# Low parts of split attention weights on VectorE, and weight buffers that live across three stages of a streaming encoder step

## Chip, cores and metric

The kernel runs on one core of a Trainium2 chip. The metric is the time of one execution on the device, in microseconds. It is given as the median of several runs; one further execution is profiled, and its rows are those quoted here.

## The reference, cut to what matters

One layer of an encoder is computed for 1024 prompt rows and 32 sample rows, width 1024. A combined projection of `h` feeds a gated DeltaNet mixer (8 heads of 128), a banded softmax attention (8 heads of 64, computed here as 4 pairs) and two gates; then come a merge, a residual norm and a mixture of experts.

```python
proj = h @ w_in
y_a = gdn_mixer(u_a, z_a, b_a, a_a, ...)          # per head, per chunk:
    # rhs = [beta * v, beta * exp(G) * k];  sol = solve(I + M, rhs)
    # q_dec = q * exp(G);  k_dec = k * exp(G_last - G)
y_b = band_attention(qb, kb, vb, rel_bias)        # softmax(q k / 8 + bias) v
mix = sigmoid(g_a) * (y_a @ w_up_a) + sigmoid(g_b) * (y_b @ w_up_b)
x = layer_norm(ALPHA * x + (1 + gt1) * (mix @ w_out))
x = layer_norm(ALPHA * x + (1 + gt2) * moe(x * (1 + sc2) + sh2))
```

The projection is made in split precision: each operand is a high part (rounded) plus a low part (operand minus high part), and a product is three matmuls, high by high, low by high, high by low.

## The kernel before

The program is a row of phases, each a block in which the five engines run their own instruction lists and at whose end they meet: entry (norm, modulation), DeltaNet (`phase_deltanet`), attention (`phase_attention`), merge (`phase_merge`), residual, dispatch, experts. Nothing of a phase starts before all engines and the awaited stores of the one before have ended.

**Projection jobs.** A weight block of 128 columns is a job. SyncE loads it into `wraw`, ScalarE rounds it into the high part (`high`), GpSimd or VectorE subtracts (`low`), and TensorE multiplies it into 3 column groups of 352 rows, 8 steps each, 24 steps in all; a step is `split_matmul` (lines 138 to 144), three matmuls. In DeltaNet `wraw` is one buffer and the pairs `w2` are two, used in turn. The list `jobs` (lines 417 to 425) has the z block of head h and the k, q, v blocks of head h + 2 in turn; the last three jobs are the blocks k, q, v of attention's pair 0. `by_vector` and `by_pool` (lines 428 to 431) say which engine subtracts which job. SyncE may load job w only when job w - 1 has been subtracted (line 556).

**A DeltaNet head.** A round h (from -1 to 7) has 9 slots, the scan of head h over 9 tiles, and beside them the preparation of head a = h + 1; then a list of 13 stages `A2` (line 434) in which TensorE multiplies 9 tiles of 128 x 128 each and VectorE or ScalarE combines the results, three tiles (384 columns) at a time. TensorE puts product steps between slots and between stages (`slot_steps`, `stage_steps`, `run(fill, n)`). In the stages VectorE takes, in this order, BT, T_V (weighted values `bv`, which is `ET`), B2, Y, W, B4, W4, the transposed outputs T_O, and QK; in BT, B2 and B4 it also squares, sums and scales the outputs of head h (lines 1132 to 1147). GpSimd makes the decayed keys `kd` and the scaled keys `kt` (`scaled_keys`, lines 779 to 789; WK needs them), the decayed queries in `WE` (`queries`, lines 791 to 796; the next scan needs them), and low parts between these.

**Attention.** For each pair, TensorE computes scores of a tile, VectorE adds the bias and takes the maximum (`soft`), ScalarE exponentiates, VectorE normalises (`norm`), TensorE transposes and multiplies by v. Beside pair p TensorE runs the products of pair p + 1, two steps at each of four places of a tile; beside the last pair it runs modulation steps instead, whose weights come through a ring of 11 buffers, 7 of them loaded early. At the start ScalarE copies the transposed v in three parts and rounds a weight after each (lines 1440 to 1442):

```python
for j in range(NJ):
    take_v(0, j)
    high(1, j)
```

TensorE may start the scores of tile 1 only when both maxima of tile 0 are taken (line 1509), and the transposes of a tile only when it is normalised (line 1526). GpSimd subtracts all 9 weights (lines 1460 to 1466). SyncE's list starts at line 1343: bias rows, tables of pair 0, the three weights of pair 1, caches.

**Merge.** 16 gate jobs and 16 up-projection jobs, with two raw buffers and two split pairs of their own; weights are loaded, rounded and subtracted in halves. The first product waits for the first half of job 0 (line 1745).

## Time and profile before

| | us |
|---|---|
| median of 3 runs | 2026.38 |
| lowest and highest | 2022.24, 2026.57 |
| the profiled execution, its own time | 2018.53 |
| its span, first to last instruction | 2016.7 |
| TensorE busy in the span | 1811.6 |
| VectorE busy | 1006.6 |
| ScalarE busy | 662.1 |
| GpSimd busy | 219.7 |
| mean granted TensorE clock (share of full) | 0.945 |

DeltaNet takes the span from about 69 to 876 us, attention from 876 to 1156, the merge from 1156 on. PE is TensorE's matmuls, DVE is VectorE, ACT is ScalarE, POOL is GpSimd, SP is SyncE, and SPq and POOLq their queues. Busy time is no proof of a bound: the wait in brackets behind a row says how long the engine had stood idle before it and on whose result it waited.

### The profile page before, as it was taken

Reading aid. Unit: us, or ns where it says so; the run is one execution under the profiler, and the core shown is the slowest. Engines: PE = TensorE matmul, PEld = TensorE weight load, DVE = VectorE, ACT = ScalarE, POOL = GpSimd, SP = SyncE. Lnnn points to the kernel's source line nnn. Section 1 sums busy time; section 2 is a strip of 40 time slices with the busy share of each in tenths; the row PEclk is TensorE's granted clock in tenths of the full one; section 3 lists DMA queues with packets and bytes.
Section 4 is the critical chain, followed back from the end, with each engine's and each line's share of the span. In section 5 each row is a group of like instructions: output and inputs, shape, how many; then the busy total and the mean of one; then the engine's idle time right before and its main releaser. Section 6 shows DMA issues by size and latency. Waiting matters only on the chain. (4 is left out here: it accounts for less than half of the span.)

```text
span 2016.7 us, 29278 instructions
## 1 busy us (share of the span) xinstructions
PE 1811.6 (90%) x11059; PEld 1536.6 (76%) x11060; DVE 1006.6 (50%) x2211; ACT 662.1 (33%) x1297; POOL 219.7 (11%) x180
## 2 busy tenths in 40 slices
PE   5889999999999998989998799998988957999991
PEld 2689999999999997977876399998976844444440
DVE  5555757474665757334444411124438972333336
ACT  3454444535353544234444322222111110110104
POOL 0101101120202021110000000000000001222220
PEclk8899999999999999989999999999989977999995
DMA  9311020101011020130232622113124345888766
GB/s 351 116 37 46 22 70 25 57 25 58 35 47 56 26 70 14 34 126 2 77 119 102 217 83 95 43 32 117 43 96 191 112 177 223 303 246 271 225 166 203
DMA packets 69166, 219.67 MB, mean 109 GB/s; under 512 B 8596, under 2 KB 14380, under 8 KB 64948
## 3 DMA queue, kind: packets, MB, share of 16 engines
q1 hardware_dynamic: 61412, 190.20, 26.3%
q0 software_dynamic: 7632, 27.79, 5.6%
q8 instruction: 83, 1.36, 0.3%
q14 instruction: 39, 0.32, 0.0%
HBM read 178.11 MB, written 42.48 MB: 109 GB/s over the span
## 5 line engine op out<-in xcount | busy, mean ns | idle before, releaser
L142 PE MATMUL bk<-hT_high,w_high 128*128 128x352 f32 x840 | 297.2, 354 | 1.1 <-DVE ssq L1191 1.1
L144 PE MATMUL bk<-hT_high,w_low 128*128 128x352 f32 x840 | 273.5, 326 | 0.0
L143 PE MATMUL bk<-hT_low,w_high 128*128 128x352 f32 x840 | 273.5, 326 | 0.0
L2400 PE MATMUL psU<-wgu,xgT 128*128 x400 | 178.9, 601 | 2.1 <-DVE xgT L2487 2.1
L142 PEld LDWEIGHTS bk<-hT_high,w_high 128*128 128x128 f32 x840 | 162.3, 193 | 1.5 <-DVE ssq L1191 1.2
L143 PEld LDWEIGHTS bk<-hT_low,w_high 128*128 128x128 f32 x840 | 162.3, 193 | 0.0
L144 PEld LDWEIGHTS bk<-hT_high,w_low 128*128 128x128 f32 x840 | 160.5, 191 | 0.0
L2400 PEld LDWEIGHTS psU<-wgu,xgT 128*128 128x128 f32 x400 | 76.9, 193 | 99.3 <-issue 99.3
L142 PE MATMUL pg<-hT_high,wx_high 128*128 128x352 f32 x384 | 124.7, 325 | 9.9 <-DVE wx_low L1804 9.9
L1804 DVE TENSOR_TENSOR wx_low<-wx,wx_high 128x512 fp32r<-128x512 f32 (+1 forms) x64 | 37.4, 622 | 186.2 <-ACT wx_high L1782 182.9
L143 PE MATMUL pg<-hT_low,wx_high 128*128 128x352 f32 x384 | 123.6, 322 | 0.0
L144 PE MATMUL pg<-hT_high,wx_low 128*128 128x352 f32 x384 | 123.5, 322 | 0.0
L986 DVE SCALAR_TENSOR_TENSOR f<-raw,cw,f 128x1059 f32<-128x1059 f32 x72 | 97.1, 1348 | 9.3 <-ACT f L644 8.7
L2347 POOL TENSOR_TENSOR wait_cell<-wait_cell 128x1 f32<-128x1 f32 x27 | 18.2, 672 | 666.8 <-DVE idx L2472 666.8
L2436 ACT ACTIVATE sgx<-psU 128x256 f32<-128x256 f32 x25 | 9.6, 386 | 242.0 <-PE psU L2400 242.0
L2417 PE MATMUL psD<-wdn,aTx 128*128 x192 | 87.4, 598 | 0.0
L2493 DVE TENSOR_TENSOR ab<-psU,sgx 128x256 f32<-128x256 f32 x25 | 10.6, 425 | 151.5 <-ACT sgx L2436 151.5
L142 PEld LDWEIGHTS pg<-hT_high,wx_high 128*128 128x128 f32 x384 | 72.6, 189 | 10.8 <-DVE wx_low L1804 10.8
L142 PE MATMUL pja<-hT_high,wa_high 128*128 128x352 f32 x216 | 80.2, 372 | 0.4 <-POOL wa_low L1465 0.4
L142 PE MATMUL py<-wo_high,mix_high 128*128 128x512 f32 (+1 forms) x144 | 59.0, 409 | 19.4 <-DVE wo_low L2007 11.5
L143 PEld LDWEIGHTS pg<-hT_low,wx_high 128*128 128x128 f32 x384 | 72.7, 189 | 0.0
L144 PEld LDWEIGHTS pg<-hT_high,wx_low 128*128 128x128 f32 x384 | 72.4, 189 | 0.0
(430 smaller groups left out, 4018.1 us busy)
## 6 DMA issues: line engine op xcount, KB each, us to landing
wgu<-in_w_gu SPq DMA_DIRECT2D x16, 2048.0 KB, 9.2
wraw<-in_w_gdn SPq DMA_DIRECT2D x32, 512.0 KB, 3.6
wdn<-in_w_dn SPq DMA_DIRECT2D x16, 1024.0 KB, 13.3
wm<-in_w_mod SPq DMA_DIRECT2D x8, 1024.0 KB, 8.0
tmp_x<-x SPq DMA_DIRECT2D x16, 512.0 KB, 6.1
wx<-in_w_gates SPq DMA_DIRECT2D x32, 256.0 KB, 3.8
spare<-in_w_mod SPq DMA_DIRECT2D x12, 512.0 KB, 8.6
Dm<-tmp_g_rows SPq DMA_DIRECT2D x8, 576.0 KB, 4.1
```

The lines of the kernel that those rows point to most:

```text
L142: pe.matmul(out, lh, rh, start=start, stop=False)
L143: pe.matmul(out, lh, rl, start=False, stop=False)
L144: return pe.matmul(out, ll, rh, start=False, stop=stop)
L986: ins = dve.scalar_tensor_tensor(out=f[b][:, 0:CONVW], in0=raw[b][:, k:k + CONVW], scalar=cw[:, a, b, k:k + 1], in1=f[b][:, 0:CONVW], op0= ...
L1804: dve.tensor_tensor(lo[:, half(j, h), :], raw[j % 2][:, half(j, h), :], plain(hi[:, half(j, h), :]), ALU.subtract).then_inc(w_split, 1)
L2347: pool.tensor_tensor(waits[:, 0:1], waits[:, 1:2], waits[:, 1:2], ALU.add).then_inc(pdone, 1)
L2400: mm = pe.matmul(psU[b][:, :], xgT[b][:, i, :], c.wgu[:, bass.ds(place, 1), i, :].rearrange("p a c -> p (a c)"), start=(i == 0), stop=(i = ...
L2417: mm = pe.matmul(psD[:, h * 512:(h + 1) * 512], aT[b][:, i, :], c.wdn[:, bass.ds(place, 1), i, h * 512:(h + 1) * 512].rearrange("p a c -> ...
L2436: act.activation(sg[b][:, :], psU[b][:, 0:DE], ACT.Silu).then_inc(sgd, 1)
L2493: dve.tensor_tensor(ab[b][:, :], psU[b][:, DE:2 * DE], sg[b][:, :], ALU.mult).then_inc(a, 1)
```

## The change

Four things are changed.

1. In the DeltaNet stages VectorE makes the decayed keys (in stage T_V), the scaled keys (in Y) and the decayed queries (in W4), each behind its own combination, and the low part of the third weight of a round in W. GpSimd keeps its small fills and the low part of a round's last weight.
2. DeltaNet gets one more job to prepare, not to multiply: the first weight of attention's pair 1. It is loaded, rounded by ScalarE and subtracted by GpSimd in the last round, in buffer pair `c.ahead` (35 jobs, so pair 1).
3. `wraw` and the two pairs `w2` are allocated so that they live through attention and merge; attention uses them for two of its three weights, the merge for its jobs. Attention's other low parts are VectorE's, behind `norm` and `out` of tiles 0 and 1 (pair 0) and 3, 6, 9 (pairs 0 and 1).
4. In the last pair the first gate weight is loaded into `wraw`, rounded and subtracted, in attention; the merge starts with job 1's loads. The modulation ring has 10 buffers, 6 of them loaded early.

```diff
--- before.py
+++ after.py
@@ -423,12 +423,15 @@
     NSUB = NJ * len(jobs)
+    NEXT = len(jobs)
+    c.ahead = NEXT % 2
     EARLY = 2
...
     in_slots = [first_job[h] + 1 for h in range(-1, HA - 1)]
-    in_stages = [first_job[h] + 2 for h in range(-1, HA - 1) if first_job[h] + 2 <= first_job[h + 1]]
-    by_vector = sorted(in_slots + in_stages)
-    by_pool = [w for w in range(EARLY, len(jobs)) if w not in by_vector]
+    after_stage = {"BT": 2, "W": 3}
+    by_vector = sorted(in_slots + [first_job[h] + n for h in range(-1, HA - 1) for n in after_stage.values()
+                                   if first_job[h] + n < first_job[h + 1] + (n == 2)])
+    by_pool = [w for w in range(EARLY, NEXT + 1) if w not in by_vector]
 
@@ -554,8 +557,8 @@
                         weights_split(sp, w - 1)
-                    head, b = jobs[w]
-                    sp.dma_start(wraw[:, :, :], d["w_gdn"][head, b] if head < HA else d["w_att"][0, b]).then_inc(s["w_raw"], 16)
+                    head, b = jobs[w] if w < NEXT else (HA + 1, VB)
+                    sp.dma_start(wraw[:, :, :], d["w_gdn"][head, b] if head < HA else d["w_att"][head - HA, b]).then_inc(s["w_raw"], 16)
 
@@ -572,7 +575,7 @@
                 for h in range(-1, HA):
-                    w, end = first_job[h] + 1, min(first_job[h + 1], len(jobs) - 1)
+                    w, end = first_job[h] + 1, first_job[h + 1]
                     if w <= end:
@@ -601,7 +604,7 @@
 
-                    if w >= len(jobs):
+                    if w > NEXT:
                         return
@@ -763,7 +766,7 @@
                 def low(w):
-                    if w >= len(jobs):
+                    if w > NEXT:
                         return
@@ -775,25 +778,6 @@
                     pool.memset(X[:, :, :].rearrange("p i j -> p (i j)")[:, 0:BS * BS:BS + 1], 1.0).then_inc(s["x_one"], 1)
-
-                def scaled_keys(a):
-                    evacuated(pool, a, "T_K")
-                    evacuated(pool, a, "BT")
-                    if a > 0:
-                        pool.wait_ge(s["ds"], NCHUNK * a)
-                    pool.tensor_tensor(by_tile(kd), by_tile(kt), tok(a, Q_KD).unsqueeze(2).to_broadcast([P, TILES, P]),
-                                       ALU.mult).then_inc(s["kd"], 1)
-                    pool.wait_ge(s["kd"], a + 1)
-                    pool.wait_ge(s["cols"], a + 1)
-                    pool.tensor_tensor(by_tile(kt), by_tile(kt), col[:, 2, :].unsqueeze(2).to_broadcast([P, TILES, P]),
-                                       ALU.mult).then_inc(s["kb"], 1)
-
-                def queries(a):
-
-                    pool.wait_ge(full[NGRP - 1], use[a, "W4", NGRP - 1] + 1)
-                    pool.wait_ge(s["actv"], 3 * a + 2)
-                    pool.wait_ge(s["eg_in"], 16 * (a + 1))
-                    pool.tensor_tensor(WE[:, :, P:2 * P], by_tile(f[QB]), by_tile(EG), ALU.mult).then_inc(s["eq"], 1)
 
@@ -804,13 +788,9 @@
                     blocks(a)
-                    scaled_keys(a)
-                    if w + 3 <= end:
-                        low(w + 2)
-                    queries(a)
                     if w + 2 <= end:
                         low(end)
-                for w in range(first_job[HA - 1] + 1, len(jobs)):
+                for w in range(first_job[HA - 1] + 1, NEXT + 1):
                     low(w)
@@ -1106,8 +1086,6 @@
                                                   ALU.add).then_inc(free[g], 1)
-                            if first_job[a - 1] + 2 in in_stages:
-                                low(first_job[a - 1] + 2)
                         if name == "T_V":
@@ -1129,6 +1107,22 @@
                             combine(a, "QK", PT, Dm, ALU.mult)
+                        if name == "T_V":
+                            evacuated(dve, a, "T_K")
+                            if a > 0:
+                                dve.wait_ge(s["ds"], NCHUNK * a)
+                            dve.tensor_tensor(by_tile(kd), by_tile(kt), tok(a, Q_KD).unsqueeze(2).to_broadcast([P, TILES, P]),
+                                              ALU.mult).then_inc(s["kd"], 1)
+                        if name == "Y":
+                            dve.wait_ge(s["kd"], a + 1)
+                            dve.wait_ge(s["cols"], a + 1)
+                            dve.tensor_tensor(by_tile(kt), by_tile(kt), col[:, 2, :].unsqueeze(2).to_broadcast([P, TILES, P]),
+                                              ALU.mult).then_inc(s["kb"], 1)
+                        if name == "W4":
+                            dve.wait_ge(full[NGRP - 1], use[a, "W4", NGRP - 1] + 1)
+                            dve.wait_ge(s["actv"], 3 * a + 2)
+                            dve.wait_ge(s["eg_in"], 16 * (a + 1))
+                            dve.tensor_tensor(WE[:, :, P:2 * P], by_tile(f[QB]), by_tile(EG), ALU.mult).then_inc(s["eq"], 1)
                     if h < 0:
@@ -1152,6 +1146,10 @@
                                                      in1=zs[:, lo:hi], op0=ALU.mult, op1=ALU.mult).then_inc(free[g], 1)
+
+                def stage_low(h, name):
+                    if h < HA - 1 and name in after_stage and first_job[h] + after_stage[name] in by_vector:
+                        low(first_job[h] + after_stage[name])
 
@@ -1222,6 +1220,7 @@
                         second(h, a, name)
+                        stage_low(h, name)
 
@@ -1237,8 +1236,8 @@
 
-        w = [buf(f"wa{i}", [P, KD, P]) for i in range(3)]
-        w2 = [[buf(f"wa{i}_{n}", [P, KD, P], F32R) for n in ("high", "low")] for i in range(3)]
+        w = [buf(f"wa{i}", [P, KD, P]) for i in range(2)] + [c.wraw]
+        w2 = [c.w2[1 - c.ahead], [buf(f"wa1_{n}", [P, KD, P], F32R) for n in ("high", "low")], c.w2[c.ahead]]
         qT = [c.raw[0], buf("qT1", [P, PAD])]
@@ -1260,9 +1259,9 @@
             "pj_ready", "pj_taken", "vt_ready", "vt_taken", "sc_ready", "x_ready", "p_ready", "p_norm", "pt_ready",
-            "pt_taken", "y_ready", "y_taken", "chain", "qz", "bm_in", "bm_zero", "m_step",
+            "pt_taken", "y_ready", "y_taken", "chain", "qz", "bm_in", "bm_zero", "g_in", "g_high", "m_step",
             "m_taken", "rows_out")}
-        early = [flat2(w[b][:, :, :]) for b in ORDER] + [spare[i][:, :] for i in range(4)]
+        early = [flat2(w[b][:, :, :]) for b in range(2)] + [spare[i][:, :] for i in range(4)]
         ring = early + [m[:, 0:D] for m in (qT[0], kT[0], flat2(v[0][:, :, :]), vT)]
@@ -1284,6 +1283,10 @@
             return TILES * p + t + 1
+
+        def split(p, o):
+
+            return 3 * (p - 1) + o
 
@@ -1294,8 +1297,10 @@
                     for o, b in enumerate(ORDER):
-                        if p > 1:
-                            sp.wait_ge(s["w_split"], 3 * (p - 2) + o + 1)
+                        if p == 1 and o == 0:
+                            continue
+                        if p > 1 and split(p - 1, o) > 0:
+                            sp.wait_ge(s["w_split"], split(p - 1, o))
                         sp.dma_start(w[b][:, :, :], d["w_att"][p, b]).then_inc(s[f"w{b}"], 16)
@@ -1362,7 +1367,8 @@
                     if p + 2 == PAIRS:
-                        sp.wait_ge(s["w_split"], 3 * (PAIRS - 1))
+                        sp.wait_ge(s["w_split"], split(PAIRS - 1, 2))
+                        sp.dma_start(c.wraw[:, :, :], d["w_gates"][0, 0]).then_inc(s["g_in"], 16)
                         for i in range(len(early)):
@@ -1385,7 +1391,9 @@
                     b = ORDER[o]
-                    act.wait_ge(s[f"w{b}"], 16 * p)
+                    if p == 1 and o == 0:
+                        return
+                    act.wait_ge(s[f"w{b}"], 16 * (p if o > 0 else p - 1))
                     if p > 1:
@@ -1442,6 +1450,10 @@
                     for i in range(TILES + 2):
+                        if p == PAIRS - 1 and i == TILES + 1:
+                            act.wait_ge(s["g_in"], 16)
+                            act.wait_ge(s["pj_ready"], job(p, 0, NJ - 1))
+                            act.activation(c.w2[c.ahead][0][:, :, :], c.wraw[:, :, :], ACT.Copy).then_inc(s["g_high"], 1)
                         if p + 1 < PAIRS and NJ <= i < 2 * NJ:
@@ -1457,13 +1469,6 @@
             def _(pool):
-                for p in range(1, PAIRS):
-                    for o, b in enumerate(ORDER):
-                        pool.wait_ge(s["w_high"], 3 * (p - 1) + o + 1)
-                        if p > 1:
-                            pool.wait_ge(s["pj_ready"], job(p - 1, o, NJ - 1))
-                        pool.tensor_tensor(w2[b][1][:, :, :], w[b][:, :, :], plain(w2[b][0][:, :, :]),
-                                           ALU.subtract).then_inc(s["w_split"], 1)
                 c.retire(pool)
@@ -1471,8 +1476,8 @@
                     b = ORDER[o]
-                    if j == 0:
-                        pe.wait_ge(s["w_split"], 3 * (p - 1) + o + 1)
+                    if j == 0 and (p > 1 or o > 0):
+                        pe.wait_ge(s["w_split"], split(p, o))
                     n = job(p, o, j)
@@ -1635,6 +1640,15 @@
 
+                def low(p, o):
+
+                    b = ORDER[o]
+                    dve.wait_ge(s["w_high"], split(p, o))
+                    if p > 1:
+                        dve.wait_ge(s["pj_ready"], job(p - 1, o, NJ - 1))
+                    dve.tensor_tensor(w2[b][1][:, :, :], w[b][:, :, :], plain(w2[b][0][:, :, :]),
+                                      ALU.subtract).then_inc(s["w_split"], 1)
+
                 for p in range(PAIRS):
@@ -1648,6 +1662,11 @@
                             take_mod(0)
+                        if p == PAIRS - 1 and i == TILES + 1:
+                            hi, lo = c.w2[c.ahead]
+                            dve.wait_ge(s["g_high"], 1)
+                            dve.wait_ge(s["pj_ready"], job(p, 0, NJ - 1))
+                            dve.tensor_tensor(lo[:, :, :], c.wraw[:, :, :], plain(hi[:, :, :]), ALU.subtract)
                         if i < TILES:
@@ -1655,6 +1674,10 @@
                             out(p, i - 2)
+                        if p == 0 and i in (0, 1):
+                            low(1, i + 1)
+                        if p + 2 < PAIRS and i in (NJ, 2 * NJ, 3 * NJ):
+                            low(p + 2, i // NJ - 1)
                         if p == PAIRS - 1 and i == TILES + 1:
@@ -1674,8 +1697,8 @@
     with ExitStack() as ctx:
-        raw = [sb(nc, ctx, f"wx{i}", [P, KD, P]) for i in range(2)]
-        w2 = [[sb(nc, ctx, f"wx{i}_{n}", [P, KD, P], F32R) for n in ("high", "low")] for i in range(2)]
+        raw = [c.wraw, sb(nc, ctx, "wx1", [P, KD, P])]
+        w2 = [c.w2[c.ahead], c.w2[1 - c.ahead]]
         yraw = [sb(nc, ctx, f"y_raw{i}", [P, ROWS]) for i in range(RAW_Y)]
@@ -1711,8 +1734,8 @@
                 def weights(j):
-                    if j >= 2:
-                        sp.wait_ge(w_split, 2 * (j - 1))
+                    if j > 2:
+                        sp.wait_ge(w_split, 2 * (j - 2))
                     for h in range(2):
@@ -1722,7 +1745,6 @@
 
-                weights(0)
                 weights(1)
@@ -1741,8 +1763,8 @@
                         for k in range(depth(j)):
-                            if n == 0 and k in (0, depth(j) // 2):
-                                pe.wait_ge(w_split, 2 * j + 1 + k // (depth(j) // 2))
+                            if n == 0 and j > 0 and k in (0, depth(j) // 2):
+                                pe.wait_ge(w_split, 2 * (j - 1) + 1 + k // (depth(j) // 2))
                             if n == 0 and j in lead:
@@ -1778,10 +1800,9 @@
                     for h in range(2):
-                        act.wait_ge(w_in[j % 2][h], 16 * (j // 2 + 1))
+                        act.wait_ge(w_in[j % 2][h], 16 * ((j + 1) // 2))
                         act.activation(w2[j % 2][0][:, half(j, h), :], raw[j % 2][:, half(j, h), :], ACT.Copy).then_inc(w_high, 1)
 
-                high(0)
                 high(1)
@@ -1800,11 +1821,10 @@
                     for h in range(2):
-                        dve.wait_ge(w_high, 2 * j + h + 1)
+                        dve.wait_ge(w_high, 2 * (j - 1) + h + 1)
                         dve.tensor_tensor(lo[:, half(j, h), :], raw[j % 2][:, half(j, h), :], plain(hi[:, half(j, h), :]),
...
 
-                low(0)
                 low(1)
@@ -2618,14 +2638,14 @@
             c.hT = [sb(nc, inputs, f"hT_{n}", [P, KD, ROWS], F32R) for n in ("high", "low")]
+            c.wraw = sb(nc, inputs, "wraw", [P, KD, P])
+            c.w2 = [[sb(nc, inputs, f"w{i}_{n}", [P, KD, P], F32R) for n in ("high", "low")] for i in range(2)]
             with ExitStack() as part, ExitStack() as mid:
...
                     c.ba = sb(nc, first, "ba", [P, TILES, 2 * HA])
-                    c.wraw = sb(nc, first, "wraw", [P, KD, P])
-                    c.w2 = [[sb(nc, first, f"w{i}_{n}", [P, KD, P], F32R) for n in ("high", "low")] for i in range(2)]
                     c.run(phase_entry)
```

## Rows read from the trace of the kernel before

**Rows 1.** The page, part 1: busy time, share, instructions.

```profile
PE 1811.6 (90%) x11059; PEld 1536.6 (76%) x11060; DVE 1006.6 (50%) x2211; ACT 662.1 (33%) x1297; POOL 219.7 (11%) x180
```

**Rows 2.** Stretches: middle head, attention, gates; length, busy (instructions), clock, DMA.

```profile
374.00:467.00 93.00, 90.29 (x655) 88.19 (x654) 58.40 (x125) 42.76 (x84) 14.06 (x7) 0.98 0.13 44
...
876.00:1151.00 275.00, 250.95 (x1876) 190.00 (x1876) 123.38 (x498) 127.31 (x278) 21.30 (x9) 0.96 0.32 111
...
1161.00:1345.00 184.00, 184.00 (x1151) 184.00 (x1151) 25.63 (x37) 43.41 (x84) 0.00 (x0) 0.99 0.19 62
```

**Rows 3.** Groups by line: busy us, mean ns | idle before, releaser.

```profile
L784 POOL TENSOR_TENSOR kd<-kt,tok 128x1152 f32<-128x1152 f32 x8 | 29.2, 3649 | 162.7 <-DVE UV L1107 162.7
...
L1018 DVE TENSOR_TENSOR w_low<-wraw,w_high 128x1024 fp32r<-128x1024 f32 x16 | 19.5, 1217 | 0.0
...
L1146 DVE TENSOR_TENSOR obuf<-obuf,ssq 128x1152 f32<-128x1152 f32 x8 | 10.8, 1350 | 0.9 <-ACT ssq L757 0.9
```

**Rows 4.** Timeline, a middle head: start, us, operation [idle before, releaser].

```profile
427.77 4.11 POOL L784 TENSOR_TENSOR kd<-kt,tok 128x1152 f32<-128x1152 f32 x1 [20.59 <-DVE UV L1107]
...
429.94 1.96 DVE L1113 TENSOR_TENSOR col<-tok,col 128x9 f32<-128x9 f32 x1
...
433.97 2.17 PE L847 MATMUL bk<-WE,UV 128*128 128x128 f32 x18
...
434.03 2.36 POOL L770 TENSOR_TENSOR w_low<-wraw,w_high 128x1024 fp32r<-128x1024 f32 x1
...
434.94 1.80 DVE L1099 TENSOR_TENSOR WE<-bk,WE 128x384 f32<-128x384 f32 x3 [1.30 <-PE bk L847]
...
442.25 1.90 DVE L1099 TENSOR_TENSOR UV<-bk,UV 128x384 f32<-128x384 f32 x3 [2.06 <-PE bk L847]
...
445.79 1.80 DVE L1099 TENSOR_TENSOR WE<-bk,WE 128x384 f32<-128x384 f32 x3 [1.65 <-PE bk L847]
...
452.34 1.57 DVE L1153 SCALAR_TENSOR_TENSOR yat<-bk,nw,zs 128x384 f32<-128x384 f32 x3 [1.28 <-PE bk L882]
```

**Rows 5.** Timeline, the last head that prepares a successor.

```profile
795.38 3.27 DVE L1138 TENSOR_TENSOR yat<-obuf 128x1152 f32<-128x1152 f32 x1
...
801.39 3.81 PE L847 MATMUL bk<-WE,UV 128*128 128x128 f32 x18 [1.84 <-DVE ET L1022]
```

**Rows 6.** Stretches of low clock: last preparing head; between pairs 0 and 1.

```profile
802.00:805.00 3.00, 3.00 (x16) 3.00 (x16) 1.28 (x3) 0.00 (x0) 0.00 (x0) 0.50 0.00 0
...
955.00:960.00 5.00, 5.00 (x32) 4.12 (x29) 2.96 (x18) 0.98 (x4) 0.00 (x0) 0.54 0.45 149
```

**Rows 7.** Timeline, seam from DeltaNet to attention.

```profile
879.93 1.38 SPq L1299 DMA_DIRECT2D wa<-in_w_att  x3
...
882.93 0.90 DVE L1642 COPY bias<-brev 128x640 f32<-128x640 f32 x2 [4.93 <-DMA brev<-tmp_toeplitz]
...
885.70 0.90 PE L1499 MATMUL psy<-consts,raw 128*128 128x128 f32 x3 [7.42 <-ACT v L1414]
...
886.63 1.06 ACT L1391 ACTIVATE wa_high<-wa 128x1024 fp32r<-128x1024 f32 x1 [0.99 <-DMA wa<-in_w_att]
...
890.37 0.40 ACT L1425 ACTIVATE pr<-sx,num 128x128 f32<-128x128 f32 x1
...
895.70 0.27 PE L1531 MATMUL pst<-consts,pr 128*128 128x128 f32 x1
```

**Rows 8.** Timeline, seam from attention to the merge.

```profile
1156.36 1.78 SPq L1717 DMA_DIRECT2D wx<-in_w_gates  x4
...
1160.52 0.66 PE L142 MATMUL pg<-hT_high,wx_high 128*128 128x352 f32 x1 [9.94 <-DVE wx_low L1804]
```

**Rows 9.** Timeline, a ring refill and the step that uses it.

```profile
1101.19 1.65 SPq L1331 DMA_DIRECT2D wa<-in_w_mod  x3
...
1113.65 0.62 PE L1567 MATMUL pja<-wa,silu_lanes 128*32 128x512 f32 x2
```

**Rows 10.** Loads of the modulation weights (line 1331), issue to landing.

```profile
DMA to landing us min/median/max: 4.1/8.1/10.7
```

## The prediction

> **What bounds the kernel now.** I read the page first, for the engines' shares: TensorE is busy 90% of the span, VectorE 50%, GpSimd 11% [rows 1]. Then the stretches by stage. A DeltaNet head lasts 92 to 93 us, with TensorE busy for 90.3 of 93 in a middle one; attention has TensorE busy for 251 of 275 and VectorE for 123; the gates of the merge for all of 184 [rows 2]. So these stages are TensorE's in-order stream, and the time can only move where that stream stands still. Third, what TensorE waited for and the timelines around its gaps. Three gaps are touched by this change: at the seam from DeltaNet to attention, 7.42 us [rows 7]; at the seam from attention to the merge, 9.94 us [rows 8]; and one in the last preparing head, 1.84 us [rows 5]. The chain of waits that ended last begins after the mixers, in the experts; nothing there changes, it only starts earlier or later.
>
> **Full-width operations on VectorE instead of GpSimd.** In each of 8 head preparations the two scalings of the keys and the product of queries and decay move from GpSimd to VectorE, and in 6 of them the low part of the third weight as well. GpSimd took 3.65 us for the first scaling [rows 3]; VectorE takes 1.35 us for a multiplication of this size with the same kind of broadcast operand, and 1.22 us for a low part [rows 3]. That adds 3 x 1.35 + 1.22 = 5.27 us of VectorE a head. All of it lies between tiles of stages in which TensorE has product steps to fill with. I place them in the timeline of a middle head [rows 4]: the first scaling goes into the 1.30 us that VectorE waits in front of B2, the second into the 2.06 us in front of W, the low part into the 1.65 us in front of B4, the queries into the 1.28 us in front of the transposed outputs. 1.35 is 0.05 over 1.30 and 0.07 over 1.28, but a combination that starts 0.07 late is still taken in by the product steps that TensorE has in front of its next stage, so I cost these at nothing. If that cover is gone, each 0.1 us over costs 0.1 us x 8. The low part waits for the high part, which was there before GpSimd's own subtraction at 434.03 [rows 4]; VectorE comes to it after 444. SyncE's next weight load, and behind it the state and output stores of the head, now wait for that subtraction to end at some 445.4 instead of 436.4. The state buffer is needed again only by the next head's scan, which comes after the transposed outputs at 452.34 and four more stages [rows 4], so this is hidden too.
>
> What goes away is more interesting. In that same head a 9-element product on VectorE (the line of `col`, 128x9) took 1.96 us and ended at 431.90, just when GpSimd's first scaling ended, at 427.77 + 4.11 = 431.88 [rows 4]. In the last preparing head the square of the outputs took 3.27 us, where VectorE takes 1.35 for that size, beside the same GpSimd operation [rows 3, 5]. So the engines hold each other up, and the added 1.35 us is paid with 1.8 us of stall that is removed. In middle heads TensorE does not wait there. In the last preparing head it did: 1.84 us in front of B2 for the weighted values, and then its 18 matmuls took 3.81 us with the granted clock at 0.50, that is 1.2 GHz [rows 5, 6], against 2.17 us for the same 18 at full clock [rows 4]. Without the stall the values are there before TensorE is. Gain 1.84 + 1.64 = 3.5 us; bounds 1.5 (the clock falls all the same) and 4. In one other head the same 3.27 us stall may have cost some 0.4 us, which I leave out.
>
> **Seam from DeltaNet to attention.** Before, ScalarE rounded the first attention weight between two copies of v; the load was issued at 879.93, so TensorE stood until 885.70 [rows 7]. Now this weight is split in the stage before, one more load behind an otherwise idle SyncE, 1.06 us of ScalarE and some 2.4 us of GpSimd (as at 434.03 [rows 4]), all begun once the last but one product of the phase is done, so some 10 us before its end. TensorE began that wait at 885.70 - 7.42 = 878.3 [rows 7]; one copy of v is 0.5, so its third group of transposes starts at 878.8 and its first scores are done by 879.8. Then it has 8 product steps without a wait; a step is 3 matmuls, 3 x 184/1151 = 0.48 us [rows 2], so it is done at 883.7. The second scores need the first softmax maximum: bias tables arrive at 882.93 [rows 7], two copies and four memsets take 1.6 us and the two maxima 0.9, so 885.5. Four more steps end at 887.9. The next tile's transposes need the exponential: ScalarE must still round the last weight. The second load landed at 886.63 and a rounding takes 1.06 us [rows 7], then 1.28 us of table load and 0.4 to 0.6 us of exponential, and 0.5 us on VectorE: 890.1, against 895.70 before [rows 7]. TensorE has then done the same 12 steps, 5.6 us sooner. The low part of the second weight, 1.22 us, now stands on VectorE in front of the second tile's maximum, and costs TensorE some 0.7 us. Gain 5.0 us; bounds 3 and 6. Low in it: the twelve steps run at half the clock, as the 18 matmuls of rows 5 did after a wait of 1.84 us. Eight steps then end at 879.8 + 7.7 = 887.5 and four more, behind 0.5 us of scores, at 891.8, 1.7 us after the probabilities are there. I take full clock, since in rows 5 the stream before the wait was thin too, and here it was full up to the seam.
>
> The Trainium skill, in "TensorE: Matmul & The Clock Gate", Part 1, calls the throttled state the default, which only activity releases. By that rule this seam, now in pieces of work and wait instead of one long wait, stays at the low clock through its first steps, and the gain here is the 3.3 us of the low case, the sum 10.9 us. No run here shows it yet.
>
> The other 8 low parts of attention lie behind the last operation of a tile, where VectorE waits for the next scores (it is busy 123 of 275 us [rows 2]), so they are hidden. The ring of modulation loads loses one of 11 buffers: a buffer freed by step n is needed by step n + 5. The first refill can go out at 1101.2 and the step needing it starts at 1113.65 [rows 9], 12.5 us, against 8.1 us median and 10.7 us worst landing [rows 10]. Hidden.
>
> **Seam from attention to merge.** The first gate weight is split while the last tile is finished: 1.06 us on ScalarE behind its last copy of the tile, 1.22 us on VectorE, while TensorE multiplies the last values and ends the modulation, at 1160.52 - 9.94 = 1150.6 [rows 8]. VectorE is free of it before that, so nothing is late. TensorE's first product then needs only the phase to begin: SyncE's first load of the merge goes out at 1156.36, TensorE began at 1160.52 [rows 8]. Gain 4.1 us. The second weight arrives as the first did, near 1160, and is needed after 24 steps, 11.5 us. The idle time before it remains 5.8 us, and the clock will be at 1.2 GHz as before for the first steps. Bounds 3 and 4.5.
>
> **Sum.** 3.5 + 5.0 + 4.1 = 12.6, say 13 us. Against the profiled execution, 2018.5 us (span 2016.7 and 1.8 around it), this is 2006; but the median of the three runs is 2026.4, 8 us more. The forecast for a median is 2026.4 - 13 = 2013.4. Elsewhere the clock drops by the luck of the moment: 0.54 between 955 and 960 us, where TensorE's matmuls follow each other without a gap [rows 6]. One such stretch more or less is worth (1 - 0.54) x 5 = 2.3 us there, and I allow 3 for the part outside those 5 us.
>
> **Rivals.**
> (a) Only half: the last head's gain stays out, or the softmax chain holds TensorE at the first seam, so that a gain at one place is lost. 12.6 - 5 - 1.5 = 6 us: 2020. For it: ScalarE's first exponential moves from 890.37 to 889.0 only [rows 7]. Against it: TensorE's steps in front of that chain are then done, where before they stood in the way of the next scores. Chance 0.17.
> (b) No change: TensorE arrives sooner at waits that other engines or loads set (the saturated loads of attention, a lower clock in two stretches more). 12.6 less 2 x 3 and 3 for the loads leaves 3.6: 2023. Against it: the gates stage has no wait at all. Chance 0.12.
> (c) Slower: VectorE becomes the bound between the tiles of the DeltaNet stages. Its free time there is 1.30 + 2.06 + 1.65 + 1.28 = 6.3 us [rows 4] for 5.27 us added, and TensorE's next stage follows at once. Beyond an uncovered (12.6 + 4)/8 = 2.1 us a head the kernel is slower; all 5.27 uncovered would give 42 - 13 = 29 us: 2055. Half, 21 - 13 = 8 us: 2034. Against it: the placement above fits within 0.1 us each. Chance 0.05.
> That the change does not do what it says: a split for attention's first weight that comes after the phase began would leave that seam as it was; it has 10 us, and I count it in (a).
>
> **How the numbers follow.** The forecast holds 0.66. A measurement here tells 0.2% (4 us) from no change. (a) and the forecast are faster: 0.83; (b) is the same: 0.12; (c) slower: 0.05. The range: largest gain 6 + 4.5 + 4 + 3 for one low-clock stretch gone = 17.5, 2009, and the runs of before alone spread by 4 us: 2005. Smallest: (a) with one stretch added, 6 - 3 = 3: 2023, where (b) also lies. 2005 to 2022.
>
> **What would show it.** In the changed kernel: VectorE's `col` product near 0.2 us and the output squares at 1.35 in every head; no wait before B2 in the last preparing head and a clock of 1.00 in it; TensorE idle under 1 us before attention's third transposes; the first tile's probabilities transposed some 20 us after the last DeltaNet matmul became 14.5; 5.8 us between modulation and first gate matmul in place of 9.94. I am wrong if middle heads grow past 92.5 us, if TensorE waits for a VectorE stage combination more than 0.2 us, or if attention's modulation steps wait for loads.

## The result, and the profile after

The changed kernel takes 2009.1 us (median of 4 runs, 2006.94 to 2009.89) against 2026.47 us of the kernel before (4 runs, 2022.24 to 2027.67): ratio 0.9916, 95% interval 0.9899 to 0.9933. The gain is 17.4 us where 13 were forecast. The two profiled executions, 2009.89 and 2018.53 us (spans 2008.0 and 2016.7), differ by only 8.7 us. Why the two gains, 8.7 and 17.4 us, differ is the main lesson of the case.

The page, part 1, of the changed kernel, against [rows 1]: GpSimd gave up 102 us, VectorE took on 28.

```profile
PE 1809.5 (90%) x11059; PEld 1536.8 (77%) x11060; DVE 1034.3 (52%) x2248; ACT 662.0 (33%) x1296; POOL 117.8 (6%) x142
```

The stretches of [rows 2]. VectorE is busier by 2.7 us in a middle head and TensorE's time is the same: the added work is hidden, as forecast.

```profile
374.00:467.00 93.00, 90.33 (x654) 88.26 (x653) 61.14 (x127) 42.79 (x84) 2.86 (x3) 0.98 0.13 44
876.00:1151.00 275.00, 248.89 (x1870) 189.32 (x1870) 131.33 (x505) 126.28 (x276) 0.00 (x0) 0.96 0.32 113
1161.00:1345.00 184.00, 184.00 (x1159) 184.00 (x1158) 28.06 (x42) 43.16 (x86) 0.00 (x0) 1.00 0.16 51
```

VectorE's timeline in a middle head, against [rows 4]: `col` takes 0.16 us, not 1.96, and the first scaling goes in front of the combinations of B2, with no wait of TensorE for it.

```profile
429.02 1.35 DVE L1132 TENSOR_TENSOR yat<-obuf 128x1152 f32<-128x1152 f32 x1
430.40 1.23 DVE L998 TENSOR_TENSOR w_low<-wraw,w_high 128x1024 fp32r<-128x1024 f32 x1
431.54 0.16 DVE L1091 TENSOR_TENSOR col<-tok,col 128x9 f32<-128x9 f32 x1
433.75 1.49 DVE L1002 TENSOR_TENSOR ET<-bk,col 128x384 f32<-128x384 f32 x3 [2.04 <-PE bk L830]
435.15 1.35 DVE L1114 TENSOR_TENSOR kd<-kt,tok 128x1152 f32<-128x1152 f32 x1
```

The last preparing head, against [rows 5, 6] (TensorE's timeline and a window): no wait, 2.17 us in place of 3.81, full clock.

```profile
800.16 2.17 PE L827 MATMUL bk<-WE,UV 128*128 128x128 f32 x18
...
797.00:806.00 9.00, 8.31 (x67) 8.03 (x66) 7.83 (x15) 1.27 (x4) 0.00 (x0) 1.00 0.00 0
```

The change also brings one new hold-up. In the last round, which prepares no head, the square of the outputs now takes 2.47 us instead of 1.36, because GpSimd subtracts the weight prepared ahead beside it. TensorE runs product steps without a wait there (858 to 873 us), so it costs nothing.

```profile
861.94 2.47 DVE L1132 TENSOR_TENSOR yat<-obuf 128x1152 f32<-128x1152 f32 x1 [0.17 <-ACT obuf L735]
...
860.80 2.39 POOL L773 TENSOR_TENSOR w_low<-wraw,w_high 128x1024 fp32r<-128x1024 f32 x1 [12.72 <-ACT w_high L612]
```

The seam from DeltaNet to attention, against [rows 7]. The v transposes no longer wait for a weight, but there is a new wait of 4.80 us: ScalarE copies the first product result (L1412), from the only PSUM buffer that the products have, after two weights and two exponentials.

```profile
882.74 0.70 PE L1526 MATMUL sc<-raw 64*128 64x256 f32 x4 [1.65 <-DVE num L1618]
888.24 0.66 PE L142 MATMUL pja<-hT_high,w_high 128*128 128x352 f32 x1 [4.80 <-ACT raw L1412]
...
883.23 1.06 ACT L1399 ACTIVATE w_high<-wa 128x1024 fp32r<-128x1024 f32 x1 [7.17 <-DMA wa<-in_w_att]
...
884.61 1.04 ACT L1399 ACTIVATE wa_high<-wa 128x1024 fp32r<-128x1024 f32 x1
885.67 1.28 ACT L1433 ACT_TABLE_LOAD   x1
886.96 0.40 ACT L1433 ACTIVATE pr<-sx,num 128x128 f32<-128x128 f32 x1
...
887.75 0.44 ACT L1412 ACTIVATE raw<-pja 128x352 f32<-128x352 f32 x1
```

The seam from attention to the merge, against [rows 8]: 5.80 us of wait where there were 9.94, and what is left is the beginning of the phase itself. The window behind it has the clock at 1.2 GHz for its first steps.

```profile
1151.49 0.63 PE L142 MATMUL pg<-hT_high,w_high 128*128 128x352 f32 x1 [5.80 <-PEq L1295]
...
1151.00:1155.00 4.00, 3.51 (x12) 3.54 (x13) 0.20 (x1) 0.86 (x2) 0.00 (x0) 0.51 0.49 160
```

### The profile page after: what moved, and what is told of

Its sections match the earlier page's. It is cut to its first block and busy times, and to the rows that moved or that the text cites. A ratio compares the mean times of both kernels' runs of the same rounds, so it can differ in the third digit from the quotient of the medians.

```text
span 2008.0 us, 29270 instructions
## 1 busy us (share of the span) xinstructions
PE 1809.5 (90%) x11059; PEld 1536.8 (77%) x11060; DVE 1034.3 (52%) x2248; ACT 662.0 (33%) x1296; POOL 117.8 (6%) x142
## 3 DMA queue, kind: packets, MB, share of 16 engines
q8 instruction: 83, 1.36, 0.3%
## 5 line engine op out<-in xcount | busy, mean ns | idle before, releaser
L142 PE MATMUL pg<-hT_high,w_high 128*128 128x352 f32 x384 | 124.7, 325 | 5.8 <-PEq L1295 5.8
L143 PE MATMUL pg<-hT_low,w_high 128*128 128x352 f32 x384 | 123.8, 322 | 0.0
L144 PE MATMUL pg<-hT_high,w_low 128*128 128x352 f32 x384 | 123.5, 322 | 0.0
L142 PEld LDWEIGHTS pg<-hT_high,w_high 128*128 128x128 f32 x384 | 72.6, 189 | 6.7 <-issue 6.7
L143 PEld LDWEIGHTS pg<-hT_low,w_high 128*128 128x128 f32 x384 | 72.7, 189 | 0.0
L144 PEld LDWEIGHTS pg<-hT_high,w_low 128*128 128x128 f32 x384 | 72.5, 189 | 0.0
L1433 ACT ACTIVATE pr<-sx,num 128x640 f32<-128x640 f32 (+5 forms) x72 | 50.6, 703 | 54.1 <-DVE num L1618 51.4
L1825 DVE TENSOR_TENSOR w_low<-wx,w_high 128x512 fp32r<-128x512 f32 (+1 forms) x32 | 18.7, 621 | 95.8 <-ACT w_high L1804 92.5
```

Of the source, the lines that this page charges most:

```text
L142: pe.matmul(out, lh, rh, start=start, stop=False)
L143: pe.matmul(out, lh, rl, start=False, stop=False)
L144: return pe.matmul(out, ll, rh, start=False, stop=stop)
L1433: act.activation(pr[tile(p, t) % 2][e][:, 0:nk], x[e][:, 0:nk], ACT.Exp, scale=SCALE, bias=num[:, e, 1:2], accum_out=num[:, e, 2:3]).then_ ...
L1825: dve.tensor_tensor(lo[:, half(j, h), :], raw[j % 2][:, half(j, h), :], plain(hi[:, half(j, h), :]), ALU.subtract).then_inc(w_split, 1)
```

## The experiments

All were timed beside runs of the kernel before on the same chip: 2024.94 us (median) beside e1 to e4, 2021.57 beside e5 to e8, 2023.35 beside e9 to e11, 2025.16 beside e12. In the tables and texts, "DeltaNet" is the stretch from the first to the last matmul start of that stage (PSUM tile `bk`) in the profile; "turn" and "attention" are the times from that last matmul to the first transposition of probabilities and to the last modulation matmul, "seam to merge" from there to the first gate matmul.

### Splitting the change: e1, e2, e3

e1 is the kernel before, unchanged. e2 has only the change in the DeltaNet stages; e3 has everything but that (first weight of attention and first weight of the gates split ahead, low parts in attention on VectorE). So e2 is the kernel before with this, and e3 the changed kernel without it:

```
 (GpSimd)
-                    scaled_keys(a)
-                    if w + 3 <= end:
-                        low(w + 2)
-                    queries(a)
 (VectorE, in second and behind it)
+                        if name == "T_V":      # kd
+                        if name == "Y":        # kt
+                        if name == "W4":       # WE, the queries
+                        stage_low(h, name)
```

> The kernel before, unchanged, profiled a second time. The question is why its median is 8 us above its profiled execution (2026.4 against 2018.5) when the changed kernel's profiled execution lies on its median. Theory A (contention between GpSimd and VectorE varies from run to run): a run at the median has the long stall, 3.27 us for the output squares, in more than 2 of 8 heads, and DeltaNet, 806 us from its first matmul to its last in the profile before, grows to 810 or more. Theory B (granted clock): the time is lost in stretches at clock 0.5, the stalls are as before. Theory C (elsewhere, as loads in entry or experts): DeltaNet and attention last as before. Time: ratio 1.000 to the kernel before, within 0.2%.

> The kernel before with only the move inside the DeltaNet stages: scaled keys, decayed queries and the third weight's low part on VectorE; no weight prepared over a seam, attention's low parts still on GpSimd. Theory of the prediction: 3.5 us faster than before, from the last preparing head alone, both seams as before (7.4 and 9.9 us). Rival (the contention costs in more heads in ordinary runs): 8 to 12 us faster. Rival (VectorE becomes the bound): no gain or a loss, with TensorE waits on stage combinations.

> The changed kernel with the DeltaNet stages as before (GpSimd scales the keys and makes the third low part), both seams with the prepared weights. From the two traces: 1.0 us at the first turn of attention, 1.1 more to the end of attention and 4.1 us at the merge, so 5 to 7 us faster than the kernel before. The prediction had 9 us for the two seams. If the ordinary gain of 17 us comes from the seams, this gains over 12.

| run | median us | ratio (95%) | DeltaNet | turn | attention | seam to merge |
|---|---|---|---|---|---|---|
| before, first profile | 2026.47 | | 805.8 | 20.4 | 274.7 | 10.5 |
| e1 | 2026.05 | 1.0001 (0.9991 to 1.0011) | 810.4 | 23.4 | 275.4 | 10.5 |
| e2 | 2015.86 | 0.9955 (0.9939 to 0.9972) | 800.1 | 23.5 | 274.6 | 10.5 |
| e3 | 2017.89 | 0.9965 (0.9952 to 0.9977) | 811.0 | 19.1 | 270.9 | 6.4 |
| after | 2009.1 | 0.9916 (0.9899 to 0.9933) | 801.1 | 19.4 | 272.5 | 6.4 |

Against 2024.94 the stages bring 9.1 us (forecast 3.5) and the seams 7.1 (forecast 9.1); 16.2 together, near the 17.4 of both. So the theory of the prediction fell in e2 and its rival of 8 to 12 us held; e3 came out at the top of its 5 to 7. e1 shows why the stages are worth more: the same program takes 810.4 us for the DeltaNet stages in this profile and took 805.8 in the first, as its theory A said. The waits of TensorE in those stages have the reason, first e1, then the first profile of before; the changed kernel has no such row.

```profile
PE bk L847 <- DVE ET L1022: 4.0, 6, 1.8
```

```profile
PE bk L847 <- DVE ET L1022: 2.3, 2, 1.8
```

Six waits against two. They go with the length of the square of the outputs on VectorE: 3.27 us in 6 of 7 heads of e1 and of e3, in 2 of 7 of the first profile, in none of e2. Two timelines of the same program side by side, first the middle head of the first profile around [rows 4], then the same head in e1:

```profile
427.43 1.22 DVE L1018 TENSOR_TENSOR w_low<-wraw,w_high 128x1024 fp32r<-128x1024 f32 x1
...
428.56 1.35 DVE L1138 TENSOR_TENSOR yat<-obuf 128x1152 f32<-128x1152 f32 x1
```

```profile
429.70 1.21 DVE L1018 TENSOR_TENSOR w_low<-wraw,w_high 128x1024 fp32r<-128x1024 f32 x1
430.83 3.27 DVE L1138 TENSOR_TENSOR yat<-obuf 128x1152 f32<-128x1152 f32 x1
434.14 1.96 DVE L1113 TENSOR_TENSOR col<-tok,col 128x9 f32<-128x9 f32 x1
...
430.04 2.85 POOL L784 TENSOR_TENSOR kd<-kt,tok 128x1152 f32<-128x1152 f32 x1 [20.58 <-DVE UV L1107]
432.97 3.11 POOL L788 TENSOR_TENSOR kt<-kt,col 128x1152 f32<-128x1152 f32 x1
```

Read as turns, every duration falls into place. In e1 GpSimd's first scaling (430.04) waits for the low part to end (430.91) and then holds the square: it ends at 432.89, the square 1.2 us later, at 434.10. GpSimd's second scaling, started at 432.97, waits for the square and takes 2.0 us from there, to 436.08, and `col` waits for that: 436.10. In the first profile the square followed the low part at once, GpSimd's scaling waited for both (4.11 us [rows 4]), and only `col` was held. In both, the scaling starts 0.34 us behind the low part. Which form a head takes is thus drawn at the moment when the low part ends; over the first profile, e1 and e3 it was the long one 14 times in 21.

### A missed idea at the seam: e4

```
                 for j in range(NJ):
                     take_v(0, j)
+                    if j == NJ - 1:
+                        take(1, 0, 0)
                     high(1, j)
```

(and the take left out of the first tile).

> The changed kernel, with one more edit: at the start of attention ScalarE takes the first result of the prepared product before it rounds the last weight, and not after the first exponentials. Theory: the one PSUM buffer for products held TensorE at the seam (4.8 us wait on that copy), and the gain of 5 us that was predicted for the seam is lost to it. Then the wait is under 1 us, the first tile's probabilities are transposed 3 to 4 us sooner after the last DeltaNet matmul (19.1 us in the changed kernel, now 15 to 16), and the time is 3 to 4 us below the changed kernel, about 2005.5. Rival: the softmax chain (loads, roundings, table load, exponential) sets that point anyway; then under 1 us.

It took 2009.27 us, ratio 0.9924 (0.9905 to 0.9944): nothing gained beside the changed kernel's 0.9916, where 3 to 4 us were expected. The turn came at 16.0 us instead of 19.4, and TensorE's wait of 4.80 us fell to 1.62, but attention took 271.3 against 272.5 us. Most of what the first turn won was lost at the second transposition, in front of which there is a new wait for ScalarE. The second transposition came 19.4 us after the last DeltaNet matmul, against 20.5 in the changed kernel:

```profile
888.95 0.27 PE L1539 MATMUL pst<-consts,pr 128*128 128x128 f32 x1
...
892.34 0.30 PE L1539 MATMUL pst<-consts,pr 128*128 128x128 f32 x1 [2.15 <-ACT pt L1442]
```

ScalarE still stood in a wait for a load (7.15 us), then did two roundings ahead of the exponentials.

### Which operation holds which: e5, e6

e5 is e3 with the first scaling alone on VectorE, e6 the changed kernel with the first scaling alone back on GpSimd; both move this operation and its waits:

```
e5  (GpSimd)  -  pool.tensor_tensor(by_tile(kd), ...)
    (VectorE) +  if name == "T_V": dve.tensor_tensor(by_tile(kd), ...)
e6  (VectorE) -  if name == "T_V": dve.tensor_tensor(by_tile(kd), ...)
    (GpSimd)  +  pool.tensor_tensor(by_tile(kd), ...)
```

e8 is the changed kernel again, their yardstick.

> The kernel with both seams changed (as in e3), and of the DeltaNet stages only the first scaling of the keys (kd) on VectorE; the second scaling, the queries and the third low part stay on GpSimd. Theory A, the stall is made by that one operation, which meets the col product and the square of the outputs: squares of 1.35 us in all 7 heads, col near 0.2 us, the stretch from the end of the entry to the end of the DeltaNet stages 801 to 803 us, span near 2009, ratio to before 0.992. Theory B, every two-input GpSimd operation holds up whichever two-input VectorE operation runs beside it, so the collision only moves on: the second scaling, now from about 436.5 us in a middle head, stretches the stage combinations, TensorE waits for one of them in each head, the DeltaNet stages stay at 806 to 810 us, ratio 0.995 to 0.997.

> The changed kernel, but the first scaling of the keys goes back to GpSimd; the other three operations stay on VectorE. Theory A: the square takes 3.27 us in 6 of 7 heads (2 of 7 by luck), DeltaNet stages 806 to 810 us, ratio to before 0.9965, all of e2's gain lost. Theory B or a theory of total GpSimd load: about a quarter to a half of GpSimd's work is back, so a quarter to a half of 9 us is lost, 2011 to 2014 us, ratio 0.993 to 0.995.

> The changed kernel unchanged, beside the others on the same chip: 2009 us, ratio 0.9916 within 0.002; no square of the outputs over 1.5 us, DeltaNet stages 801 us. The yardstick for e5 to e7.

e5 2009.91 us, ratio 0.9941 (0.9926 to 0.9955); e6 2009.53, 0.9936 (0.9921 to 0.9951); e8 2009.86, 0.9938 (0.9924 to 0.9952). DeltaNet stages 802.0, 801.1 and 802.3 us. Theory A held for e5 and fell with e6: with the first scaling on GpSimd there is still a hold in each of 7 heads, on the low part, and no time is lost. Theory B fell in both: TensorE waits for no stage combination in e5, and e6 takes no longer than e8. VectorE and GpSimd in a middle head of e6:

```profile
427.37 1.35 DVE L1135 TENSOR_TENSOR yat<-obuf 128x1152 f32<-128x1152 f32 x1
428.75 3.02 DVE L1007 TENSOR_TENSOR w_low<-wraw,w_high 128x1024 fp32r<-128x1024 f32 x1
431.69 0.15 DVE L1100 TENSOR_TENSOR col<-tok,col 128x9 f32<-128x9 f32 x1
432.09 1.49 DVE L1011 TENSOR_TENSOR ET<-bk,col 128x384 f32<-128x384 f32 x3 [0.24 <-PE bk L839]
...
427.71 2.98 POOL L787 TENSOR_TENSOR kd<-kt,tok 128x1152 f32<-128x1152 f32 x1 [20.59 <-DVE UV L1096]
```

One hold of 1.8 us is free here; TensorE waits only where two stand in a row in front of B2. Taking the first scaling off GpSimd is enough (e5), and so is taking off the second together with the queries and the third low part (e6). These last two, which e5 left on GpSimd, cost nothing there. The second scaling was not moved by itself. e5 also shows which VectorE operations are not held. Beside GpSimd's second scaling and low part run combinations with one operand in PSUM and a reduction, all at their usual length, while a 9-element product of two SBUF operands ends with GpSimd's low part (441.35), 1.39 us in place of 0.17:

```profile
436.88 1.80 DVE L1095 TENSOR_TENSOR WE<-bk,WE 128x384 f32<-128x384 f32 x3
438.60 1.34 DVE L1142 TENSOR_REDUCE ssq<-yat 128x9 f32<-128x1152 f32 x1
439.98 1.39 DVE L1143 SCALAR_TENSOR_TENSOR ssq<-ssq,qe 128x9 f32<-128x9 f32 x1
...
436.92 2.12 POOL L784 TENSOR_TENSOR kt<-kt,col 128x1152 f32<-128x1152 f32 x1 [27.82 <-DVE kd L1132]
438.99 2.36 POOL L772 TENSOR_TENSOR w_low<-wraw,w_high 128x1024 fp32r<-128x1024 f32 x1
```

The ratio 0.9938 of e8 beside 0.9916 of the first comparison comes from the kernel before, 2021.57 us on that chip; the changed kernel's own medians are 2009.86 and 2009.1. Why the kernel before was faster there is open: it was not profiled on that chip. In e8, too, the square in the last round takes 2.47 us, where its expectation had none over 1.5.

### The seam with ScalarE in another order: e7, e10, e11

```
-                    high(1, j)
+                take(1, 0, 0)
...
+                            if p == 0 and i in (0, 1):
+                                high(1, i + 1)
...
-                        if p == 0 and i in (0, 1):
-                            low(1, i + 1)
+                        if p == 0 and i in (1, 2):
+                            low(1, i)
```

> The changed kernel; at attention's beginning ScalarE takes the first product result as soon as it stands, then does the first exponentials, and rounds the second and third weight only behind them; their low parts go one tile later on VectorE. If the end of this seam is set by ScalarE's order (the v copies behind the wait for the load at 883.2 us, and two roundings ahead of the exponentials), the first probabilities are turned 11 to 13 us after the last DeltaNet matmul instead of 19.3, with no 0.50 clock in that stretch, attention ends 5 to 7 us sooner, ratio to before 0.988 to 0.990, 2003 us. If what the start of attention saves is given back in the saturated rest of it (as e4's 3 us seemed to be), attention ends less than 2 us sooner: 2008, ratio 0.991 to 0.992.

> The changed kernel with e7's order, and two steps more: SyncE fetches the bias tables ahead of the modulation's bias rows, and ScalarE does the first exponentials ahead of the first product's copy. If the seam is still set by the chain tables, maxima, table load, exponentials, the first turn comes 10 to 11.5 us after the last DeltaNet matmul, against 13.1 in e7, and the kernel is 1 to 2.5 us shorter than e7, near 2000 us. If the product's copy, now later, holds TensorE instead, the turn stays at 13 us and the time at e7's.

> e7 unchanged, beside e10 on the same chip: 2002 us within 2; first turn 13.1 us after the last DeltaNet matmul, attention's end 265 us after that.

The `take` that stood in the first tile is left out, as in e4. The first theory of e7 held: it took 2001.9 us, 0.9904 (0.9888 to 0.992), where e8 on the same chip has 2009.86: 8.0 us less than the changed kernel. Turn 13.1 us, attention 264.9 against 272.4. ScalarE and TensorE there, and a window with full clock; the changed kernel's mean clock from 876 to 896 us is 0.83, and e7 has no stretch at 0.50 between 770 and 1076 us:

```profile
878.28 0.46 ACT L1412 ACTIVATE raw<-pja 128x352 f32<-128x352 f32 x1 [3.95 <-PE pja L144]
878.76 1.28 ACT L1433 ACT_TABLE_LOAD   x1
880.05 0.40 ACT L1433 ACTIVATE pr<-sx,num 128x128 f32<-128x128 f32 x1
...
880.11 0.70 PE L1529 MATMUL sc<-raw 64*128 64x256 f32 x4 [1.87 <-DVE num L1621]
...
876.00:892.00 16.00, 14.13 (x85) 11.29 (x84) 10.21 (x45) 9.80 (x23) 0.00 (x0) 1.00 0.78 263
```

e11 repeats it: 2001.73 us, 0.9896 (0.9882 to 0.991), turn 12.6. e10, which is e7's order with the tables fetched first and the exponentials ahead of the copy, has the turn at 11.1 us as expected, but attention takes 265.1: 2000.65 us, 0.9895 (0.988 to 0.991), no difference from e11 that can be measured. Both are faster than either kernel of the case. Where e10's 1.5 us went was not followed up by a run: TensorE idles 1.1 us less in its attention than in e11's, and loses 1.7 us more to low clock (6.8 against 5.1, summed as one minus the granted clock over all windows).

### The hold-up by itself: e9, e12

```
-                    pool.tensor_tensor(by_tile(kd), by_tile(kt), tok(a, Q_KD)..., ALU.mult)
+                    pool.tensor_scalar(by_tile(kd), by_tile(kt), 0.5, None, ALU.mult)
```

(the same for the second scaling.)

> The kernel before, in which GpSimd's two scalings of the keys read one operand in SBUF (a multiplication of 128x1152 by the constant 0.5) instead of two; the place, the order and the waits stay. The scaling by the decays and by col is left out of the computation. Theory C, drawn from e5 and e6: an operation of GpSimd with two operands in SBUF and one of VectorE with two operands in SBUF don't run at the same time, the later waits for the whole of the earlier. Then nothing is held here: col 0.17 us, the square 1.35 us in 7 of 7 heads, the DeltaNet stages 801 to 803 us instead of 806 to 811, and 5 to 9 us less than before. Theory D, any work of GpSimd in SBUF holds VectorE up: col stays near 2 us, some squares over 2 us, and the time is that of before, 2021 to 2026 us.

2059.04 us, ratio 1.0186 (1.0163 to 1.0209). Theory C fell: one SBUF operand on GpSimd's side is enough. Four of 7 heads have the long form.

```profile
432.91 4.05 DVE L1136 TENSOR_TENSOR yat<-obuf 128x1152 f32<-128x1152 f32 x1
437.00 2.73 DVE L1111 TENSOR_TENSOR col<-tok,col 128x9 f32<-128x9 f32 x1
...
432.14 3.85 POOL L784 TENSOR_SCALAR kd<-kt 128x1152 f32<-128x1152 f32 x1 [20.63 <-DVE UV L1105]
436.07 3.88 POOL L787 TENSOR_SCALAR kt<-kt 128x1152 f32<-128x1152 f32 x1
```

Theory D's time missed too: this form is some 0.9 us longer on GpSimd, so the holds grew, TensorE waited 8.6 us for ET in 5 places, and the DeltaNet stages took 818.7 us. Four of these waits, 1.95 to 1.99 us, are in the long heads. The fifth, 0.70 us, is in the last preparing head, which has the short form: a single hold is free only up to a length, and 2.6 us was too long there. Another 23 us over e1 lie in the experts (304.4 us from the first to the last matmul into `psU` against 281.4, with 432 of them against 400), which this kernel feeds with other values; they say nothing of the hold.

e12 is the kernel before with the square put ahead of the low part:

```
 (name == "BT", in front of the square)
-                            if first_job[a - 1] + 2 in in_stages:
-                                low(first_job[a - 1] + 2)
 (behind second(h, a, name))
+                        if name == "BT" and h < HA - 1 and first_job[h] + 2 in in_stages:
+                            low(first_job[h] + 2)
```

> The kernel before, with one exchange on VectorE: the square of the outputs goes ahead of the low part that stood in front of it. In the three profiles of that order, GpSimd's first scaling reached its turn just as the 1.22 us low part ended, and either it or the square went next (17 times of 21 profiled heads counted below as long or short). Theory L, each of the two engines waits for the whole operation of the other, and the long form costs TensorE time because then two holds (by the first and by the second scaling) stand in front of B2: with the 1.35 us square in front, GpSimd comes later within it and gets the turn behind it every time, as in e6: the low part takes 3.0 us and col 1.9 us in 7 of 7 heads, TensorE waits for ET in about 6 of 7 heads, DeltaNet stages 810 to 812 us, the time 2024 to 2028 us with a narrow spread, ratio to before 1.000 to 1.002. Rival: in e6 there was no wait because the low part is the operation held instead of the square; then this order alone gives e6's 801 us and 0.995.

(The count in it is wrong: 14 of 21 heads were long.) 2026.42 us, ratio 1.0006 (0.9997 to 1.0015); the low part takes 3.02 us and `col` 2.07 in the middle head, TensorE waits for ET 7 times, 4.4 us in all, the DeltaNet stages take 811.8 us.

```profile
432.03 3.02 DVE L1018 TENSOR_TENSOR w_low<-wraw,w_high 128x1024 fp32r<-128x1024 f32 x1
434.97 2.07 DVE L1111 TENSOR_TENSOR col<-tok,col 128x9 f32<-128x9 f32 x1
...
434.05 2.98 POOL L788 TENSOR_TENSOR kt<-kt,col 128x1152 f32<-128x1152 f32 x1
```

Eleven runs lie within 3.7 us (2024.52 to 2028.22), where fifteen of the kernel before on that chip lie within 7.5 (2021.03 to 2028.51). The draw is gone, and it is gone to the long form. Theory L holds, and its rival falls: it isn't which VectorE operation is held, it is how many holds stand in a row.

## Why the prediction was right, and where it was off

**Direction and size.** 2009.1 lies in 2005 to 2022, and the forecast case came true: each of the three gaps got smaller. The rivals of no change and of VectorE as the bound did not come. Middle heads did not grow, and there is no wait for a load in the modulation's ring.

**Stages: 3.5 forecast, 9.1 measured.** The failing step is "In middle heads TensorE does not wait there". It was read from a head with the short form. The long one had been noticed in "one other head" and left out. In an ordinary run it stands in most heads. From e1 to e2 the waits for `ET` go from 4.0 us in 6 places to none, and the time lost to low clock in the DeltaNet stages (one minus the granted clock, summed) from 29.0 to 23.9 us. That is 9.1 us together. The forecast had 3.5 of it, all in the last preparing head: there e1 has the wait of 1.84 us and a stretch at 0.50 right behind it, and e2 has neither. The waits in middle heads add 2.1 us. The other 3.4 us are two more stretches at 0.50, which lie well behind a wait (from 402.7 and 590.4 us, where the waits end at 342.4 and 530.0). e1, e3 and e12, each with the long form or its like in at least 6 heads, have two such stretches more; the first profile and the kernels without the wait have none. How the holds bring them about is not shown. The sentence that the engines hold each other up was right.

**The reference.** The 8 us between the profiled execution and the median were put down to "the luck of the moment" of the clock. Between the spans of the first profile and of e1, 7.5 us, 4.6 lie in the DeltaNet stages (805.8 against 810.4), with 2 long squares against 6, another 1.7 ahead of them, and 0.8 in attention. So the profile shown was an unusually good execution of the kernel before, in part by the draw, and a gain read from it alone is too small. Of the 65 other runs of that kernel in this document only two are faster (2017.1 and 2017.35 us). The changed kernel doesn't draw, and its six runs of e8 spread by 2.8 us, against 9.2 over the eleven of the kernel before on that chip (2017.35 to 2026.56). That the draw alone makes the spread is not shown: e4, which doesn't draw either, spreads by 6.0 us in four runs.

**Seam to attention: 5.0 forecast, about 3 measured** (7.1 of e3 less the 4.1 of the other seam; attention is 4.5 us shorter in e3 than in e1, but only 2.1 shorter in the changed kernel than in e2 or the first profile). The turn came at 19.4 us where 14.5 was forecast (the forecast's own times, 890.1 less 875.3, give 14.8). Right was that the wait for v goes to zero, and the second scores at 882.74. The failing step is "Four more steps end at 887.9": these steps need the product buffer that ScalarE empties only behind its exponentials, so TensorE stood for 4.80 us, and then ran four steps at 1.2 GHz. The low case of the prediction, 3.3 us, which the Trainium skill's rule of the throttled default was said to give ("TensorE: Matmul & The Clock Gate", Part 1), is nearer to the measured size, but not by the mechanism that the prediction drew from it: the first eight steps ran at 2.4 GHz (128x352 matmuls 0.16 us apart), and in e7, with waits of up to 1.9 us between its pieces, the clock stayed at 1.00 from 872 to 896 us.

What was missing was a wait. Removing two thirds of it alone (e4) brought the turn to 16.0 us and no time that can be measured. e7 removed it together with ScalarE's wait for a load and the two roundings ahead of the exponentials: turn 13.1 us, near the forecast's 14.5, and 8.0 us less in all. In its attention TensorE idles 4.9 us less than in e8's and loses 3.4 us less to low clock. So the missing wait explains the late turn; how much of the missing 2 us it holds back by itself is open, since e4 puts it at little (attention 1.2 us shorter) and e7 changes three things at once.

A turn that comes sooner by a load's luck is not kept, though. The first profile had it 3.0 us before e1 (its first weight was rounded from 884.21, 4.3 us behind the issue [rows 7]; in e1 6.2) and ended attention only 0.8 us sooner.

**Seam to merge: 4.1 forecast, 4.1 measured** (10.5 to 6.4 in every pair), with 5.8 us left and the low clock behind it, as written.

**The sum.** 12.6 against 17.4 is in the main two errors of opposite sign: 5.6 too little for the stages, 2 too much for the first seam; the 1.2 us left are within the noise. Beside the kernel before on the chip of e5 to e8, 2021.57 us there, the gain was 11.7, so the sum lies between two measured gains. That it comes so near either is partly luck.

## What to carry to other kernels

Before pricing the removal of a stall, look at the same operation in every iteration, not in one, and ask the median of the runs whether the profiled execution was an ordinary one: here the length of one 1152-element square, 1.35 or 3.27 us, told the two forms apart. Keep GpSimd and VectorE from meeting twice in a row with SBUF operands ahead of something that TensorE needs; moving the first scaling alone was worth as much as moving all four operations. At a seam, put ScalarE's work in the order in which TensorE will miss it (free the only product buffer, exponentials, then weights for later): three moved calls brought 8 us, where freeing the buffer alone brought nothing that could be measured.

## What the runs showed of the hardware

A VectorE operation with two operands in SBUF and a GpSimd operation that reads SBUF do not overlap; the later waits for the other to end, even for a 9-element product (0.16 us alone, 1.96 held, 2.73 beside the longer form of e9). The ends agree to 0.02 us in e1; in e9 the held product ends 0.22 us before the recorded end of GpSimd's operation. The Trainium skill has this rule, in "SBUF — State Buffer", "Who interferes with whom": the pair of ports that the two share is an exclusive lock, taken by a VectorE instruction with two SBUF inputs against a GpSimd instruction that reads SBUF. The traces agree on all three sides: two operands against two (e1), two against one (e9), and no hold for a reduction or an operand from PSUM (e5). The rule says why `col` took 1.96 us and that every head is exposed, which the prediction did not draw from it.

Where a VectorE operation ends and both the next one and a waiting GpSimd operation want the turn, either got it, at starts equal to 0.01 us. With the stages as before (first profile, e1, e3), GpSimd won 14 of 21 times with 0.87 us between its start and the end of VectorE's operation; in e6 and e12, with 1.0 us, it won 7 of 7 each. Whether these 0.13 us decide it was not tested on its own.
